# Two-layer hybrid decoder on one core: S5 products on different rows and columns of TensorE, and the Mamba-2 step-size chain in PSUM

## The chip, the cores and the metric

The kernel runs on one core of a Trainium2 chip. The engines of a core run side by side, each with its own in-order list of instructions, and wait for each other on semaphores: TensorE (PE) multiplies, VectorE (DVE) and GpSimd (POOL) do elementwise work, ScalarE (ACT) does activations and copies, SyncE (SP) issues DMAs. The metric is the device time of the whole program in microseconds (us); lower is better.

## The reference, cut to what matters

```python
D_MODEL, SEQ, DEPTH = 1024, 512, 2
for l in range(DEPTH):
    h = rmsnorm(x, ln1_g[l]); proj = h @ w_in[l]
    o_a = diff_attention(q, k, v, ...)                 # 4 heads, q and k normed and rotated
    o_b = sc_b * causal_dwconv(sc_c * sc_h, sc_conv_w[l])
    o_c = s5_mixer(proj[..., OFF_S5:OFF_M2Z], ...)
    o_d = mamba2_mixer(z, xbc, dt_raw, ...)
    x = x + concat(o_a, o_b, o_c, o_d) @ w_out[l]
    h2 = rmsnorm(x, ln2_g[l])
    x = x + (silu(causal_dwconv(h2 @ ffn_w_gate[l])) * (h2 @ ffn_w_up[l])) @ ffn_w_down[l]

def s5_mixer(u, ...):                    # 16 groups of 16 channels, 64 complex states each
    bu = einsum('bsgh,gph->bsgp', u, b_bar)            # input product, real and imaginary part
    xs = associative_scan(a2*a1, a2*x1 + x2)           # along the 512 positions
    y = einsum('bsgp,ghp->bsgh', xs, c).real + d_skip * u   # output product
    g = gelu(y); return g * sigmoid(g @ w_glu + b_glu)

def mamba2_mixer(...):
    xbc = silu(causal_dwconv(xbc, conv_w) + conv_b)
    dt = softplus(dt_raw + dt_bias)                    # the step sizes: 512 positions x 4 heads
    y = ssd_chunked(xs * dt, a * dt, bm, cm); ...
```

## The kernel before, in words

Activations lie transposed: 128 channels on the partitions, 512 positions along the row. Every large product is cut into *units*: one unit is 128 output channels. Its weights are fetched by SP (`raw`), split by ACT into a high part (`wh`, line 697, `prep`) and by POOL into the rest (`wl`, line 287, `low`), and multiplied by PE in three groups of products (lines 386, 388, 396), of which the last needs `wl`. `raw`, `wh` and `wl` have two buffers each, so ACT can split the weights of a unit only when PE has read the high part of the unit two before it. A layer has 28 units of the input projection, then attention with the first output units among it, eight units for the rest of the output projection, and 60 units of the gated MLP.

The input projection is a hand-written schedule. Each engine has a loop over the step `s` from 2 (ACT from 1) to 27, where step `s` is unit `s`, and small pieces of the four mixers are put at fixed steps of each loop. What the change touches:

- **Mamba-2 convolution, steps 2 to 7.** DVE scales the unit out of its bank (line 942) and runs four taps in the bank (lines 959 to 962); ACT then applies Silu from the bank (line 790) in the same step, after `prep()`. Between them, in steps 2 to 4, DVE computes the softplus of the step sizes on tiles of 16 columns: `m2_dt`, `m2_log`, `m2_series` (lines 1019 and 1021, seven dependent operations) and `m2_steps`. All of these tiles lie in SBUF, in `s16` (`s` in the trace).
- **S5, eight steps `j`.** `s5_in(j)` on PE makes two products, real into bank 2 and imaginary into bank 3, both from the same 32 rows of `u` (line 437). DVE turns them by a cosine/sine table and scans them (`s5_scan`, lines 1130 to 1144), ACT copies both out (line 772), DVE makes the real part `sE` (`s5_back`, lines 1151 to 1160) and POOL the imaginary part `s5im` (lines 320 to 324). `s5_out(j)` on PE adds real (line 446) and imaginary (line 448) into the same 32 rows of bank 6. `s5_in(j + 1)` needs bank 2 back, that is `sE` of step `j`. POOL may write `s5im` again when PE has read it, and makes the tables (lines 301 to 311) when DVE has done with the old ones.
- **q and k, steps 17 to 24.** `qk_mean` on PE (lines 531 and 533), the reciprocal root on ACT as Ln then Exp (lines 715 and 717), `qk_finish` on DVE (lines 1260 to 1265), whose last operation frees bank 5 for the next line 533.
- **Attention, 16 steps `n`.** Scores on PE (lines 553 to 557; the two products of a pair use rows 0 to 63 and 64 to 127, and go to two banks), maxima and combination on DVE (lines 1272 to 1281), Exp on ACT (line 832). Once per head there is an Ln (line 842) and an Exp (line 846).

ACT holds one set of function tables at a time. A table load is an instruction in its list, put there when the next function isn't in the set that is loaded.

## Time and profile before

| | us |
|---|---|
| median of 3 runs | 1472.79 |
| lowest, highest | 1471.87, 1472.96 |
| the profiled execution, its own time | 1473.24 |
| its span, first to last instruction | 1471.4 |
| mean granted TensorE clock, share of full | 0.977 |

The 1.8 us between the span and the time lie around the program and are the same for both kernels. In a timeline row the first number is the start, the second the time from that start to the last end of the merged instructions; neighbouring groups of matmuls overlap a little, so what a group costs on PE is the start of the next group less its own start. A value in brackets is the idle time ahead, and who ended it. A product of fp32 operands shows as two matmuls.

### The profile page before, as it was taken

To read this page: it belongs to the slowest core of one execution; us is meant where nothing else is said; L and a number is where in the kernel's file an instruction comes from. 1 tells how busy PE (TensorE), PEld (TensorE's weight loads), DVE (VectorE), ACT (ScalarE), POOL (GpSimd) and SP (SyncE) were. 2 spreads that over 40 slices of the span, in tenths; PEclk is the share of its full clock that TensorE was granted. 3 is DMA by queue.
4 is the path that set the end of the run, shared out by engine and by line. 5 is a ranking of instruction groups with operands and counts; after the bars stand their busy time and mean duration, and the time that the engine had idled before them with its cause. 6 is when DMAs were issued, how large, how long until landed. Compare 5 with 4: busy or idle time off the path is not lost.

```text
span 1471.4 us, 15836 instructions
## 1 busy us (share of the span) xinstructions
PE 1395.4 (95%) x6116; PEld 1074.4 (73%) x6116; DVE 943.8 (64%) x1221; ACT 569.9 (39%) x805; POOL 685.7 (47%) x368
## 2 busy tenths in 40 slices
PE   3989999798999999999999999998899999999999
PEld 1777656476788888888877775665677888888887
DVE  7778887564677713777228788865657774067740
ACT  3342556456532312222333335645664332123221
POOL 1645768312444443444456456862134444444452
PEclk9999989999999999999999998998999999999999
DMA  5221111111332332323232211111123333223332
GB/s 185 71 73 58 44 53 55 36 33 33 107 101 92 111 98 87 95 91 116 85 100 72 61 55 58 52 42 33 40 54 112 99 100 118 83 86 101 104 101 97
DMA packets 33627, 117.41 MB, mean 80 GB/s; under 512 B 3728, under 2 KB 3856, under 8 KB 33552
## 3 DMA queue, kind: packets, MB, share of 16 engines
q1 hardware_dynamic: 33264, 115.35, 24.9%
q8 instruction: 49, 0.80, 0.2%
q10 hardware_dynamic: 288, 1.05, 0.2%
q14 instruction: 26, 0.21, 0.0%
HBM read 114.28 MB, written 2.10 MB: 79 GB/s over the span
## 4 chain that ended last, share of the span: by engine, by line
PE 84%; DVE 10%; ACT 3%; issue 2%; DMA 1%; POOL 1%; SPq 0%; DVEq 0%; POOLq 0%
PE bank L386 25%; PE bank L388 24%; PE bank L396 24%; PE bank L437 2%; DVE s L1021 1%; PE bank L533 1%; PE bank L448 1%; DVE ml L967 1%; PE bank L446 1%; PE bank L415 1%; PE bank L531 1%; DMA raw<-in_w_first 1%; DVE G L1281 1%; PE bank L572 1%; DVE xl L933 1%
## 5 line engine op out<-in xcount | busy, mean ns | idle before, releaser
L287 POOL TENSOR_TENSOR wl<-raw,wh 128x1024 fp32r<-128x1024 f32 (+3 forms) x208 | 501.7, 2413 | 679.5 <-ACT wh L697 458.5
L386 PE MATMUL bank<-xl,wh 128*128 128x512 f32 x1152 | 303.4, 404 | 35.8 <-ACT wh L697 24.9
L386 PEld LDWEIGHTS bank<-xl,wh 128*128 128x128 f32 x1152 | 217.8, 192 | 109.7 <-issue 39.7
L697 ACT ACTIVATE wh<-raw 128x1024 fp32r<-128x1024 f32 (+3 forms) x208 | 218.3, 1050 | 196.9 <-PE bank L388 191.2
L388 PE MATMUL bank<-xh,wh 128*128 128x512 f32 x1152 | 287.9, 392 | 0.0
L396 PE MATMUL bank<-xh,wl 128*128 128x512 f32 x1152 | 286.1, 390 | 0.0
L388 PEld LDWEIGHTS bank<-xh,wh 128*128 128x128 f32 x1152 | 218.5, 190 | 46.1
L396 PEld LDWEIGHTS bank<-xh,wl 128*128 128x128 f32 x1152 | 216.4, 188 | 45.2 <-issue 0.3
L971 DVE TENSOR_TENSOR x<-x,bank 128x512 f32<-128x512 f32 x64 | 44.0, 687 | 219.7 <-PE bank L396 219.7
L386 PE MATMUL bank<-ml,wh 128*128 128x512 f32 x512 | 136.3, 408 | 0.0
L388 PE MATMUL bank<-mh,wh 128*128 128x512 f32 x512 | 128.4, 391 | 0.0
L396 PE MATMUL bank<-mh,wl 128*128 128x512 f32 x512 | 127.5, 389 | 0.0
L386 PEld LDWEIGHTS bank<-ml,wh 128*128 128x128 f32 x512 | 97.8, 194 | 24.5 <-issue 3.0
L388 PEld LDWEIGHTS bank<-mh,wh 128*128 128x128 f32 x512 | 96.9, 189 | 20.9
L396 PEld LDWEIGHTS bank<-mh,wl 128*128 128x128 f32 x512 | 96.1, 188 | 20.0
L1303 DVE TENSOR_TENSOR G<-G 128x512 f32<-128x512 f32 x44 | 105.2, 2391 | 4.6
L893 ACT ACTIVATE G<-G 128x512 f32<-128x512 f32 x44 | 27.8, 632 | 204.4 <-DVE G L954 204.4
L949 DVE TENSOR_SCALAR G<-pad,par_all 128x512 f32<-128x512 f32 x48 | 94.3, 1964 | 1.5
L942 DVE TENSOR_TENSOR G<-bank,rbc 128x512 f32<-128x512 f32 x76 | 52.2, 687 | 63.7 <-PE bank L396 61.4
L942 DVE TENSOR_TENSOR pad<-bank,rbc 128x512 f32<-128x512 f32 x60 | 41.4, 691 | 53.9 <-PE bank L396 43.3
L896 ACT ACTIVATE mh<-G 128x512 fp32r<-128x512 f32 x44 | 27.7, 630 | 111.1 <-DVE G L1303 111.1
L1305 DVE TENSOR_TENSOR ml<-G,mh 128x512 fp32r<-128x512 f32 x44 | 47.3, 1074 | 31.2 <-ACT mh L896 31.2
(264 smaller groups left out, 1529.9 us busy)
## 6 DMA issues: line engine op xcount, KB each, us to landing
raw<-in_w_gu SPq DMA_DIRECT2D x88, 512.0 KB, 3.5
raw<-in_w_in SPq DMA_DIRECT2D x52, 512.0 KB, 3.5
raw<-in_w_dn SPq DMA_DIRECT2D x32, 704.0 KB, 4.1
raw<-in_w_oe SPq DMA_DIRECT2D x16, 384.0 KB, 3.0
raw<-in_w_ol SPq DMA_DIRECT2D x16, 256.0 KB, 2.6
x<-in_x SPq DMA_DIRECT2D x8, 256.0 KB, 6.1
raw<-in_w_first SPq DMA_DIRECT2D x4, 512.0 KB, 6.7
out_x<-x SPq DMA_DIRECT2D x8, 256.0 KB, 4.7
```

What stands on the lines that cost most here:

```text
L287: tt(wl[:, p, 0:cols], raw[:, p, 0:cols], wh[:, p, 0:cols].bitcast(F32), ALU.subtract).then_inc(wl_full, 1)
L386: mm(bank[b][:, :], wh[:, p, k * P:(k + 1) * P], lo[:, k, :], start=(k == 0), stop=False)
L388: w = mm(bank[b][:, :], wh[:, p, k * P:(k + 1) * P], hi[:, k, :], start=False, stop=False)
L396: w = mm(bank[b][:, :], wl[:, p, k * P:(k + 1) * P], hi[:, k, :], start=False, stop=(k == K - 1))
L437: mm(bank[2 + c][:, :], bmat[r:r + SH, c, j // 4, :], u[r:r + SH, j // 4, :], start=True, stop=True).then_inc(dve_bank[2 + c], 1)
L697: fn(wh[:, p, 0:cols], raw[:, p, 0:cols], ACT.Copy).then_inc(wh_full, 1)
L893: fn(G[:, 1, :], G[:, 0, :], ACT.Silu).then_inc(g_silu, 1)
L942: tt(out, bank[b][:, :], rbc[:, :], MUL).then_inc(unit_out, 1)
L949: after(ts(out, pad[:, p, 4:4 + T], weights[n - 1], None, MUL))
L971: tt(x[:, o, :], x[:, o, :], bank[p][:, :], ADD).then_inc(resid, 1)
L1303: tt(G[:, 3, :], G[:, 1, :], G[:, 2, :], MUL).then_inc(h_ready, 1)
L1305: tt(ml[:, i, :], G[:, 3, :], mh[:, i, :].bitcast(F32), SUB).then_inc(hid_ready, 1)
```

## The change

- `s5_in`: the imaginary product now reads a second copy of `u` whose partition halves are exchanged (`uswap`, two DMAs per layer on SP after step 5's weights), with `bmat` rolled to match. The two products of a step so use rows `r` and `r + 64` of the array.
- `s5_out(j)`: the real product of step `j` is followed by the imaginary product of step `j - 1`; the two write different groups of 32 rows of the bank, so use different columns of the array. `s5im` gets a second buffer. The last imaginary product stands alone behind `s5_out(7)`. Bank 7 takes the sums of `j` from 4 up. The first Gelu and the sum ahead of it go from step 21 to 23.
- The step-size chain keeps one operand of nearly every operation in PSUM (`small(i)`, columns of bank 5).
- ACT's Silu of a convolved unit stands one step later, behind the `prep()` of the next weights.
- `ln_exp_tables()` loads one set of tables with Ln and Exp at five places; the loads between each Ln and Exp are no longer in the list.

```diff
@@ sync
+                if g % (len(UNITS) // L) == 5:
+                    sp.wait_ge(unit_out, unit_out_of(l, 1))
+                    for to, of in ((0, P // 2), (P // 2, 0)):
+                        sp.dma_start(uswap[to:to + P // 2, :, :], u[of:of + P // 2, :, :]).then_inc(u_swapped, 16)
@@ gpsimd, s5_imaginary
-                if j:
-                    pool.wait_ge(s5_summed, l * SJ + j)
-                tt(s5im[:, :], sB[:, :], sn, ALU.mult)
+                if j > 1:
+                    pool.wait_ge(s5_summed, l * SJ + j - 1)
+                im = imag[j % 2][:, :]
+                tt(im, sB[:, :], sn, ALU.mult)
@@ tensor
+                    pe.wait_ge(u_swapped, 32 * (l + 1))
                 r = SH * (j % 4)
-                for c in range(2):
-                    claim(2 + c, (s5x_ready, dve_free[3])[c])
-                    mm(bank[2 + c][:, :], bmat[r:r + SH, c, j // 4, :],
-                       u[r:r + SH, j // 4, :], start=True, stop=True).then_inc(dve_bank[2 + c], 1)
+                claim(2, s5x_ready)
+                claim(3, dve_free[3])
+                for c, (rows, first) in enumerate(((u, r), (uswap, (r + P // 2) % P))):
+                    at = slice(first, first + SH)
+                    mm(bank[2 + c][:, :], bmat[at, c, j // 4, :], rows[at, j // 4, :],
+                       start=True, stop=True).then_inc(dve_bank[2 + c], 1)
...
             def s5_out(j):
...
+                if j:
+                    pe.wait_ge(s5im_ready, nth(s5im_ready))
+                s5_real(j)
+                if j:
+                    s5_imag(j - 1)
@@ scalar
+            def ln_exp_tables():
+
+                nc.scalar.preload_act_table_set("natural_log_exp_and_others")
...
-                    if 2 <= s <= 7:
+                    if 3 <= s <= 8:
                         act.wait_ge(conv_out, nth(conv_out))
-                        fn(xbc[:, s - 2, :], bank[unit_bank(s)][:, :], ACT.Silu).then_inc(xbc_silu, 1)
-                    if s == 6:
+                        fn(xbc[:, s - 3, :], bank[unit_bank(s - 1)][:, :], ACT.Silu).then_inc(xbc_silu, 1)
+                    if s == 7:
@@ vector
+            def small(i):
+
+                return bank[5][:, 32 + 16 * i:48 + 16 * i]
...
             def m2_series():
-                sq, q = [s16[:, i, :] for i in (9, 10)]
+                sq, q = s16[:, 9, :], small(2)
                 dve.wait_ge(dve_own, owned())
                 after(ts(q, sq, 1.0 / 17, None, MUL))
                 for c in (15, 13, 11, 9, 7, 5, 3):
...
-                stt(u[:, i, :], u[:, i, :], par_of(l, "s5d", i), bank[6][:, :], MUL, ADD).then_inc(y_ready, 1)
+                stt(u[:, i, :], u[:, i, :], par_of(l, "s5d", i), bank[6 + i][:, :], MUL, ADD).then_inc(y_ready, 1)
```

PE's list in the steps with q and k, before and then with the change (lines 437, 446, 448 are 449, 458, 463 in the new numbering; 531 and 533 are 554 and 556):

```order
L437 MATMUL bank<-u,bmat 128x512 x2
L386 MATMUL bank<-xl,wh 128x512 x8
L388 MATMUL bank<-xh,wh 128x512 x8
L396 MATMUL bank<-xh,wl 128x512 x8
L531 MATMUL bank<-G,cst 128x512
L533 MATMUL bank<-G,permg 128x512
L446 MATMUL bank<-s5e,cf 32x512
L448 MATMUL bank<-s5im,cf 32x512
L386 MATMUL bank<-xl,wh 128x512 x8
```

```order
L449 MATMUL bank<-u,bmat 128x512
L449 MATMUL bank<-uswap,bmat 128x512
L395 MATMUL bank<-xl,wh 128x512 x8
L397 MATMUL bank<-xh,wh 128x512 x8
L405 MATMUL bank<-xh,wl 128x512 x8
L554 MATMUL bank<-G,cst 128x512
L556 MATMUL bank<-G,permg 128x512
L458 MATMUL bank<-s5e,cf 32x512
L463 MATMUL bank<-s5i,cf 32x512
L395 MATMUL bank<-xl,wh 128x512 x8
```

The places and the number of products are the same; the second of each pair reads another tile, and the imaginary one (`s5i` is the second buffer of `s5im`) is that of the step before.

ACT's list in steps 1 to 4 of the input projection, before and after (697 is `prep`, 787 the exponential of the step sizes, 790 Silu; now 722, 818, 821):

```order
L697 ACTIVATE wh<-raw 128x1024 x2
L787 ACTIVATE s_102<-s_102 128x16
L790 ACT_TABLE_LOAD
L790 ACTIVATE xbc<-bank 128x512
L697 ACTIVATE wh<-raw 128x1024
L790 ACTIVATE xbc<-bank 128x512
L697 ACTIVATE wh<-raw 128x1024
L790 ACTIVATE xbc<-bank 128x512
```

```order
L722 ACTIVATE wh<-raw 128x1024 x2
L818 ACTIVATE s_104<-s_104 128x16
L722 ACTIVATE wh<-raw 128x1024
L821 ACT_TABLE_LOAD
L821 ACTIVATE xbc<-bank 128x512
L722 ACTIVATE wh<-raw 128x1024
L821 ACTIVATE xbc<-bank 128x512
```

One more split of weights now stands ahead of the first Silu, and so ahead of each later one.

## Rows read from the trace of the kernel before

**Rows 1.** The page, busy time and share of the span of each engine.

```profile
PE 1395.4 (95%) x6116; PEld 1074.4 (73%) x6116; DVE 943.8 (64%) x1221; ACT 569.9 (39%) x805; POOL 685.7 (47%) x368
```

**Rows 2.** Timeline of PE: start, us, instructions, idle before; layers 0 and 1.

```profile
80.61 3.78 PE L386 MATMUL bank<-xl,wh 128*128 128x512 f32 x8 [4.20 <-ACT wh L697]
...
799.05 3.66 PE L386 MATMUL bank<-xl,wh 128*128 128x512 f32 x8 [2.66 <-ACT wh L697]
```

**Rows 3.** Stretches: length, busy of PE, PEld, DVE, ACT, POOL; granted clock, DMA.

```profile
80.60:86.80 6.20, 6.20 (x16) 4.88 (x17) 5.95 (x9) 1.54 (x2) 4.22 (x2) 0.58 0.29 87
...
188.00:262.00 74.00, 74.00 (x252) 45.99 (x251) 57.47 (x80) 41.25 (x49) 59.92 (x43) 0.95 0.15 48
```

**Rows 4.** Timeline of ACT: the Silu ahead of the weight split that PE waited for.

```profile
79.01 0.60 ACT L790 ACTIVATE xbc<-bank 128x512 f32<-128x512 f32 x1 [11.37 <-DVE bank L962]
```

**Rows 5.** Lines 1021 and 961 on DVE: minimum, median, maximum in ns.

```profile
L1021 DVE SCALAR_TENSOR_TENSOR s<-s x14: 174/973/2424, 68.0 to 793.2; 128x16 f32<-128x16 f32 x14
...
L961 DVE SCALAR_TENSOR_TENSOR bank<-pad,par_all,bank x24: 754/756/757, 56.9 to 809.2; 128x512 f32<-128x512 f32 x24
```

**Rows 6.** Timeline of PE: the S5 products in steps 22 to 24, layer 0.

```profile
237.40 1.04 PE L446 MATMUL bank<-s5e,cf 128*32 128x512 f32 x2
238.28 1.02 PE L448 MATMUL bank<-s5im,cf 128*32 128x512 f32 x2
239.24 2.11 PE L386 MATMUL bank<-xl,wh 128*128 128x512 f32 x8
...
246.62 1.98 PE L437 MATMUL bank<-u,bmat 32*128 32x512 f32 x4
248.53 2.11 PE L386 MATMUL bank<-xl,wh 128*128 128x512 f32 x8
```

**Rows 7.** Timeline of PE: attention scores, 384 and 128 columns, and what follows.

```profile
287.37 0.92 PE L553 MATMUL bank<-qk 64*128 64x384 f32 x4
288.12 0.39 PE L555 MATMUL bank<-qk 64*128 64x128 f32 x4
...
313.83 0.49 PE L553 MATMUL bank<-qk 64*128 64x128 f32 x4
314.16 0.39 PE L555 MATMUL bank<-qk 64*128 64x128 f32 x4
```

**Rows 8.** Timeline of PE, layer 0, steps 18 and 19.

```profile
185.42 2.08 PE L533 MATMUL bank<-G,permg 128*128 128x512 f32 x2 [2.14 <-DVE qk L1265]
187.43 3.78 PE L437 MATMUL bank<-u,bmat 32*128 32x512 f32 x4
191.14 3.78 PE L386 MATMUL bank<-xl,wh 128*128 128x512 f32 x8
```

**Rows 9.** Timeline of DVE: ahead of 185 us, and the S5 real part of step 23.

```profile
177.15 3.38 DVE L967 TENSOR_TENSOR ml<-xbc,mh 128x512 fp32r<-128x512 f32 x2 [1.55 <-ACT mh L726]
180.46 2.85 DVE L1260 SCALAR_TENSOR_TENSOR qk<-G,par_all,rotary 128x512 f32<-128x512 f32 x1
...
245.19 0.69 DVE L1160 TENSOR_TENSOR s5e<-s5a,bank 128x512 f32<-128x512 f32 x1
```

**Rows 10.** Line 715 on ACT: the table loads, 22 of 84 in all.

```profile
L715 ACT ACT_TABLE_LOAD  x22: 1283/1283/1283, 45.3 to 1114.7; - x22
```

**Rows 11.** Timeline of PE: end of the projection, layer 0.

```profile
278.50 1.04 PE L448 MATMUL bank<-s5im,cf 128*32 128x512 f32 x2 [1.76 <-POOL s5im L324]
280.39 0.80 PE L553 MATMUL bank<-qk 64*128 64x128 f32 x4 [0.84 <-DVE u L1164]
```

**Rows 12.** Timeline of POOL, the same stretch.

```profile
274.61 1.27 POOL L320 TENSOR_TENSOR s5im<-s5b,ex 128x512 f32<-128x512 f32 x1 [11.64 <-PE bank L448]
```

**Rows 13.** Timeline of ACT: the last copy that POOL needs there.

```profile
270.77 0.60 ACT L772 ACTIVATE s5b<-bank 128x512 f32<-128x512 f32 x1 [0.51 <-DVE bank L1144]
```

**Rows 14.** Timeline of PE in attention, layer 0, at two head boundaries.

```profile
324.96 0.44 PE L563 MATMUL bank<-cst,G 128*128 128x128 f32 x2 [1.59 <-DVE G L1281]
...
343.06 0.44 PE L563 MATMUL bank<-cst,G 128*128 128x128 f32 x2 [1.61 <-DVE G L1281]
...
346.16 0.90 PE L563 MATMUL bank<-cst,G 128*128 128x128 f32 x3 [1.09 <-DVE G L1281]
```

More of the change, by code:

```diff
@@ L135, in build @@
         s5im = sb("s5im", [P, T], at=offsets["xds"])
+        imag = (s5im, s5im2)
         hst = sb("hst", [P, NQ - 1, M2H, M2P])
@@ L323, in s5_imaginary @@
                 pool.wait_ge(s5w_read, l * SJ + j + 1)
-                tt(s5im[:, :], s5im[:, :], s5t[:, :], ALU.add).then_inc(s5im_ready, 1)
+                tt(im, im, s5t[:, :], ALU.add).then_inc(s5im_ready, 1)
                 temp_free.append((s5im_ready, l * SJ + j + 1))
@@ L994, in dt_scaled @@
                 freed(dve_free[5])
+            def small(i):
+                return bank[5][:, 32 + 16 * i:48 + 16 * i]
             def m2_dt(l):
-                a, e = [s16[:, i, :] for i in (0, 1)]
+                a, e, raw_dt = s16[:, 0, :], s16[:, 1, :], small(0)
                 by_head = [P, NQ, M2H]
                 dve.wait_ge(dve_bank[5], nth(dve_bank[5]))
-                tt(a.rearrange("p (a b) -> p a b", a=NQ), bank[5][:, 0:16].rearrange("p (a b) -> p a b", a=NQ),
-                   par_of(l, "dtb", 0, M2H).unsqueeze(1).broadcast_to(by_head), ADD).then_inc(dve_free[5], 1)
-                dve.wait_ge(dve_free[5], freed(dve_free[5]))
-                stt(e, a, -1.0, a, MUL, ALU.max).then_inc(dt_abs, 1)
-                own(ts(a, a, 0.0, None, ALU.max))
+                for out in (a, raw_dt):
+                    w = tt(out.rearrange("p (a b) -> p a b", a=NQ), bank[5][:, 0:16].rearrange("p (a b) -> p a b", a=NQ),
+                           par_of(l, "dtb", 0, M2H).unsqueeze(1).broadcast_to(by_head), ADD)
+                after(w)
+                stt(e, raw_dt, -1.0, a, MUL, ALU.max).then_inc(dt_abs, 1)
+                dve.wait_ge(dt_abs, l + 1)
+                own(ts(a, raw_dt, 0.0, None, ALU.max))
             def m2_log():
-                e, s, sq, rec = [s16[:, i, :] for i in (1, 2, 9, 11)]
+                e, s, sq, rec = s16[:, 1, :], s16[:, 2, :], s16[:, 9, :], small(1)
                 dve.wait_ge(dt_exp, nth(dt_exp))
@@ L1012, in m2_log @@
                 after(nc.vector.reciprocal(rec, rec))
[L1013 to L1014 removed]
+                tt(s, e, rec, MUL)
+                after(tt(rec, e, rec, MUL))
+                own(tt(sq, rec, s, MUL))
             def m2_series():
[L1017 removed]
+                sq, q = s16[:, 9, :], small(2)
                 dve.wait_ge(dve_own, owned())
@@ L1023, in m2_steps @@
             def m2_steps():
-                a, s, q = [s16[:, i, :] for i in (0, 2, 10)]
+                a, s, q = s16[:, 0, :], s16[:, 2, :], small(2)
                 by_head = [P, NQ, M2H]
@@ L1028, in m2_steps @@
                 after(stt(q, q, 1.0, s, ADD, MUL))
-                after(stt(a, q, 2.0, a, MUL, ADD))
+                stt(a, q, 2.0, a, MUL, ADD).then_inc(dve_free[5], 1)
+                dve.wait_ge(dve_free[5], freed(dve_free[5]))
                 stt(adt.rearrange("p (a b) -> p a b", a=NQ), a.rearrange("p (a b) -> p a b", a=NQ), -1.0,
```

35 lines of the change are left out of this document (23 added, 12 removed).

## The prediction

> **What bounds the kernel now.** I read the page first: PE is busy for 95% of the span and no other engine for more than 64% [rows 1]. So time is won only where PE works less, waits less, or runs at a higher clock. Next I listed PE's idle gaps over the whole span in its timeline. Outside the first 31 us they lie at the same places in both layers: one ahead of 80.61 us (4.20 us; 2.66 us in layer 1) [rows 2], one of 1.7 near 147 (DVE's work on unit 13; nothing in the change touches it), two ahead of 185.42 [rows 8], the end of the projection [rows 11], and attention [rows 14]. After the long ones the granted clock is at its lower level for a while, 1.2 instead of 2.4 GHz: 0.58 of full speed on average from 80.6 to 86.8 [rows 3]. The MLP units have none of these gaps and are left out. Between 188 and 262 us PE has no gap at all, while DVE is busy for 57.5 and POOL for 59.9 of 74 us [rows 3]: there PE's own work counts, as long as the other two keep up.
>
> **The gap at 80.61: chain in PSUM, Silu one step later.** PE waits for ACT's split of its weights; ahead of that ACT had stood 11.37 us for the convolution, to run the Silu at 79.01 [rows 4]. DVE was late because of the series of line 1021. Its operations on 16 columns take 174 ns at best and 973 ns in the median, 2424 at worst, while the 512-column taps of line 961, which have one operand and the result in PSUM, take 754 to 757 ns in all 24 cases, with POOL busy beside them [rows 5]. A tiny operation slower than a 32 times larger one waits for something, and the row that is immune has only one SBUF operand. So I take 0.2 us for each of the seven, about 5 us less on DVE per layer. The Silu move gives another unit of room (5.5 us: 7.38 from 239.24 to 246.62 less two fp32 products of 0.9 [rows 6]) even without this. I count the whole gap, 4.20, and what the low clock costs: the 6.2 us from 80.6 ran at a mean clock of 0.58 [rows 3], and are 3.6 at full, so 2.6. Layer 1: 2.66, and one group of 8 products at 3.66 [rows 2] against 1.98 elsewhere, so 1.7. Together **11.1 us**. Next late would be DVE's own 4.6 us per unit, still under PE's 5.5. The later Silu holds a bank for some us longer, but four banks rotate here.
>
> The rule behind this is in the Trainium skill, page "SBUF — State Buffer", section "Who interferes with whom": a DVE instruction with two SBUF inputs contends with a GpSimd instruction that reads SBUF, one with at most one doesn't. By that rule the chain also stops holding POOL up. The trace agrees as far as the two groups of durations go.
>
> **Input products.** Four matmuls of line 437 occupy PE from 246.62 to 248.53, 1.91 us [rows 6]. The nearest row of two products on different rows of the array is that of the scores: four matmuls of 384 columns take 0.75 us (287.37 to 288.12), of 128 columns 0.33 (313.83 to 314.16) [rows 7]. A fp32 product of 512 columns costs 0.88 alone (237.40 to 238.28 [rows 6]), so 0.22 per 128 columns: in turn, 384 columns would take 1.3. They do overlap. From 0.33 and 0.75 the line goes on to 0.96 at 512 columns, so a pair saves 1.91 - 0.96 = 0.95 us. That row has 64 rows of the array and not 32; the bounds are 0 and 0.95, and I take 0.95, since the structure is the same (two row groups, two banks). Which of the eight pairs of a layer count: the one at 163.8 not (DVE is the bound right behind it, below); that at 187.43 runs at the low clock, 3.78 us [rows 8], and saves half, some 1.85; the other six 0.95 each. That makes 7.55 per layer, **15.1 us**.
>
> **Output products.** Real and imaginary of one step share the same 32 columns of the array now, 0.88 and 0.96 us (237.40, 238.28, 239.24 [rows 6]). With the change they use different columns. No row of before has two products side by side on different columns: 0 to 0.86 saved per pair. I take 0.86, because the row pairs overlap fully. Pairs that count: those of j = 2 to 5, so 3.44, and the first call at 128 us, which now issues one product instead of two, 0.86. The pair of j = 1 is lost in front of 185.42. That is 4.3 per layer, **8.6 us**. The Trainium skill, page "TensorEngine Tiling (Array Packing)", section "Key Properties", has a rule that speaks against both: to change the tiling mode drains the engine. The rows show something of the kind now: the eight products of line 386 take 2.11 us behind small ones [rows 6], and 1.98 elsewhere. By the rule this stays, since the switches are as many as before; by the rows too.
>
> **What must keep up.** `s5_in` needs `sE` of the step before: line 1160 ends at 245.88 (245.19 + 0.69 [rows 9]), PE comes at 246.62: 0.74 us of room, while a period of two units is to shrink by 1.8 us. But DVE is late there by ACT, which runs two table loads of 1.283 us around each Ln [rows 10]; 54 of 84 loads go, two of them here, 2.57 us. That turns the room into about 1.5 us over the first period, and it doesn't shrink afterwards, as DVE's scan starts from PE's product and moves with it. POOL's work in a period of 18.5 us is 15.0 (59.9 of 74 [rows 3]) against 16.7 of PE then, and it no longer waits for PE's reading of `s5im`.
>
> **Steps 16 to 18.** PE's wait of 2.14 us [rows 8] and one of 1.5 ahead of it hang on one chain: m2_norm, Ln and Exp on ACT, then DVE to line 1265. DVE spends 3.38 on two operations of line 967 and 2.85 on line 1260 [rows 9], all with two SBUF operands beside a busy POOL; these stay. Of the chain one load goes, 1.28. PE arrives 3 us earlier than now but waits the longer: **2.6 us** for two layers, low clock kept.
>
> **End of the projection.** Line 448 waits 1.76 us for POOL, which could start only at 274.61 when PE had read the buffer [rows 11, 12]; ACT had copied the data by 271.37 [rows 13]. With two buffers POOL ends near 275.2. Then bank 2 is next: scores can't start before `sE` of the last step, 274.5. From there: scores, v turn, pair (0.98), last imaginary (0.9), sum on DVE, scores at about 278.5 instead of 280.39 [rows 11]: 1.9 per layer, **3.8 us**.
>
> **Attention.** ACT loads tables ahead of and behind each Ln (2.57 us), and PE waits for what follows: 1.59 us at the first boundary, which goes whole, and 1.61 and twice 1.09 at the last [rows 14]. Those 3.8 us become about 2.3, since maxima and exponentials of the next scores take their time anyway. That is 1.59 + 1.5 = 3.1 per layer, **6.2 us**. I leave the low clock behind it as it is.
>
> **Priced at nothing**: the two uswap DMAs (issued in step 5, needed in step 10; what SP waits for, unit 1's output, is written before step 2, so no weights are held back), the Gelu two steps later, bank 7 for half of the sums (free from step 16), one more operation of 0.2 us on DVE.
>
> **Sum.** 11.1 + 15.1 + 8.6 + 2.6 + 3.8 + 6.2 = 47.4. From the profiled 1473.24 that gives 1425.8; the median is 0.45 below the profiled execution, so **1425.5 us**.
>
> **Rivals.**
> - *Low-clock stretches in attention and at the projection's end go too* as the gaps ahead of them shrink (3.4 us of loss behind 346 in each layer, as much around 282 and 998): 8 to 10 us more, 1416; with those behind 185 also, 10 more, 1406. Against: gaps of 2.6 us in 4 were enough at 277 to 280.
> - *Columns don't overlap*: 8.6 and some 1.7 at the end come back, 1435.8. For: no row shows it. Against: rows of the array do overlap.
> - *DVE or POOL becomes the bound in steps 18 to 26*: three input pairs and four output pairs per layer are lost, 2 x (2.85 + 3.44) = 12.6, so 1438. For: the 0.74 us of room, and that lines 1260 and 967 lengthen beside POOL. Against: the freed table loads.
> - *Rows don't overlap for 32-row products*: 15.1 back, 1440.6.
> - *Slower*: POOL, freed from waiting, runs beside every line 1260 (2.85 instead of 0.74 [rows 9]); DVE's period then passes 18.5 us, PE gets a gap per period, and each drops the clock as at 185 (10 us, loss 5). With four such in each layer, 40 us, and the 12.6 lost: 1478. It decides from 4 us more DVE time in each period than now.
>
> **How the numbers follow.** Forecast 0.50, low clock gone 0.18, columns 0.13, DVE or POOL 0.12, rows 0.04, slower 0.02, and 0.01 for gains that cancel out. The range, 1408 to 1440, holds all but the last three and the far end of the first rival. A measurement of this kernel can tell 0.2%, 2.9 us, from no change: faster 0.97, same 0.01, slower 0.02.
>
> **What would show it.** No gap ahead of unit 7 near 76 us in either layer, and the counterpart of line 1021 at 0.2 us; the input pair at 0.96 us and the output pair at 0.98 instead of 1.91 and 1.84; a PE without gaps and with periods of 16.7 us between 190 and 250; a longer single wait ahead of line 533 at the start of that; 30 table loads in all. A gap ahead of `s5_in` in steps 20 to 26 would prove the engines' rival, an output pair of 1.8 us that of the columns. The forecast falls if gains pass PE but come back as waits for DVE.

## The result, and the profile after

| | before | after |
|---|---|---|
| median, us | 1472.74 | 1415.13 |
| lowest, highest of 4 runs each | 1471.87, 1472.96 | 1414.43, 1416.61 |
| span of the profiled execution | 1471.4 | 1414.8 |
| mean granted TensorE clock | 0.977 | 0.990 |

The ratio is 0.9611, with a 95% interval of 0.9595 to 0.9628: 57.6 us less. The forecast was 1425.5 in a range from 1408 to 1440, so 47.4 of those 57.6 us were seen ahead, and 10.2 us weren't.

The page of after, busy time of each engine and share of the span:

```profile
PE 1352.1 (96%) x6116; PEld 1057.2 (75%) x6116; DVE 920.0 (65%) x1225; ACT 500.5 (35%) x751; POOL 685.4 (48%) x368
```

Against [rows 1], PE has the same 6116 instructions and is busy for 43.3 us less: pairs that overlap, and less time at the low clock. ACT has 54 instructions fewer, the table loads.

**The step-size chain.** The seven operations of the series (line 1061 now), with minimum, median and maximum in ns, where they take 174/973/2424 in [rows 5]:

```profile
L1061 DVE SCALAR_TENSOR_TENSOR bank<-bank,s x14: 182/182/182, 67.2 to 758.6; 128x16 f32<-128x16 f32 x14
```

PE has no idle time left ahead of unit 7 in either layer, where [rows 2] have 4.20 and 2.66 us.

**The pairs.** Timeline of PE of after, steps 21 to 23 of layer 0 (start, time to the last end, instructions):

```profile
212.95 0.69 PE L449 MATMUL bank<-u,bmat 32*128 32x512 f32 x1
212.96 0.69 PE L449 MATMUL bank<-uswap,bmat 32*128 32x512 f32 x1
213.48 0.59 PE L449 MATMUL bank<-u,bmat 32*128 32x512 f32 x1
213.49 0.59 PE L449 MATMUL bank<-uswap,bmat 32*128 32x512 f32 x1
214.01 2.14 PE L395 MATMUL bank<-xl,wh 128*128 128x512 f32 x8
...
221.43 0.62 PE L458 MATMUL bank<-s5e,cf 128*32 128x512 f32 x1
221.44 0.62 PE L463 MATMUL bank<-s5i,cf 128*32 128x512 f32 x1
221.88 0.59 PE L458 MATMUL bank<-s5e,cf 128*32 128x512 f32 x1
222.41 2.11 PE L395 MATMUL bank<-xl,wh 128*128 128x512 f32 x8
...
229.81 0.69 PE L449 MATMUL bank<-u,bmat 32*128 32x512 f32 x1
```

The first matmuls of the two products start 10 ns apart, and so do the second ones. An input pair takes 1.06 us (212.95 to 214.01) instead of 1.91, an output pair 0.98 (221.43 to 222.41) instead of 1.84 [rows 6]. The period of two units is 16.86 us (212.95 to 229.81), where it was 18.52.

**What PE waits for now.** PE of after has ten waits of more than 0.7 us between the startup and 330 us. Three of them lie outside what the change aims at (0.96 us ahead of 116.38, 1.67 ahead of 140.15, 1.77 ahead of 252.66); the other seven, with the idle time ahead and what ended it in brackets:

```profile
174.15 1.13 PE L556 MATMUL bank<-G,permg 128*128 128x512 f32 x2 [2.34 <-DVE qk L1306]
176.07 1.15 PE L449 MATMUL bank<-u,bmat 32*128 32x512 f32 x1 [0.80 <-DVE s5e L1201]
255.27 0.49 PE L578 MATMUL bank<-qk 64*128 64x128 f32 x4 [1.00 <-DVE s5e L1201]
258.35 1.05 PE L463 MATMUL bank<-s5i,cf 128*32 128x512 f32 x2 [0.94 <-POOL s5i L333]
260.32 0.49 PE L576 MATMUL bank<-qk 64*128 64x128 f32 x4 [0.93 <-DVE u L1205]
270.15 0.49 PE L578 MATMUL bank<-qk 64*128 64x128 f32 x4 [1.68 <-ACT G L864]
319.85 0.55 PE L586 MATMUL bank<-cst,G 128*128 128x128 f32 x3 [1.23 <-DVE G L1322]
```

The wait at step 18 is the longest one: 2.34 us where [rows 8] have 2.14. Of the waits at head boundaries [rows 14] only one of 1.23 us is left.

**Where the 57.6 us went.** The starts of the same piece of work in both timelines cut each layer into segments. The startup differs by 0.8 us between the two profiled executions (it ends anywhere between 35.7 and 37.7 us in the kernels here), and is taken out.

| segment of a layer | layer 0 | layer 1 | both | forecast, both |
|---|---|---|---|---|
| up to the first turn of Mamba-2 (gap ahead of unit 7) | 6.9 | 4.6 | 11.5 | 11.1 |
| on to the S5 input product of step 16 | 1.9 | 2.0 | 3.9 | 5.5 |
| on to that of step 18 | 3.3 | 3.2 | 6.5 | 2.6 |
| on to that of step 26 | 7.2 | 7.0 | 14.2 | 16.3 |
| on to the scores | 1.6 | 1.5 | 3.1 | 5.7 |
| attention, up to the second norm | 9.0 | 9.2 | 18.2 | 6.2 |

The MLP has the same length in both (360.3 us from the second norm of layer 0 to the first of layer 1). Four rows are within 0.4 to 2.6 us of their term; step 16 to 18 gave 3.9 us more, and attention 12.0 more. The two rows that say why, PE's busy time and the granted clock in attention: length, PE, PEld, DVE, ACT, POOL busy, clock, DMA share, GB/s. Before:

```profile
280.40:396.30 115.90, 105.33 (x539) 80.48 (x540) 71.37 (x127) 70.23 (x141) 27.68 (x17) 0.93 0.18 55
997.00:1113.60 116.60, 106.51 (x538) 80.95 (x539) 71.92 (x128) 70.25 (x140) 28.29 (x18) 0.91 0.19 54
```

And after:

```profile
260.30:367.20 106.90, 100.33 (x539) 77.45 (x540) 69.36 (x127) 59.93 (x133) 27.69 (x17) 0.97 0.20 59
950.00:1057.00 107.00, 100.41 (x538) 77.52 (x539) 69.48 (x128) 60.08 (x132) 27.93 (x17) 0.97 0.19 59
```

For the same matmuls PE is idle for 6.6 us instead of 10.6 in layer 0, 4.0 less (the forecast had 3.1), and busy for 5.0 us less, at a clock of 0.97 instead of 0.93. In layer 1 it is 3.1 less idle (the stretch of before begins 0.4 us earlier in a wait, which is taken out) and 6.1 less busy. So 7.1 us are waits, and 11.1 are matmuls that no longer run at 1.2 GHz. Before had three stretches at 1.2 GHz in each layer there, in layer 0 from 280.3 (the projection's end), 294.0 and 345.4 (the last head boundary); after has only the middle one, from 271.9. The place of the first one in layer 0, before and after:

```profile
280.00:287.00 7.00, 6.61 (x29) 3.97 (x29) 4.29 (x12) 5.18 (x9) 1.98 (x2) 0.76 0.38 115
260.00:267.00 7.00, 6.04 (x31) 3.29 (x33) 4.39 (x12) 5.41 (x10) 1.83 (x2) 1.00 0.42 115
```

### The profile page after: what moved, and what is told of

The parts are those of the page before. It is cut to its first block, busy times and chain, and to the rows that moved or that the text cites. A ratio compares the mean times of both kernels' runs of the same rounds, so it can differ in the third digit from the quotient of the medians.

```text
span 1414.8 us, 15816 instructions
## 1 busy us (share of the span) xinstructions
PE 1352.1 (96%) x6116; PEld 1057.2 (75%) x6116; DVE 920.0 (65%) x1225; ACT 500.5 (35%) x751; POOL 685.4 (48%) x368
## 4 chain that ended last, share of the span: by engine, by line
PE 89%; DVE 7%; ACT 1%; issue 1%; DMA 1%; POOL 1%; SPq 0%; DVEq 0%; POOLq 0%
PE bank L395 26%; PE bank L397 26%; PE bank L405 26%; PE bank L449 1%; PE bank L595 1%; PE bank L458 1%; PE bank L424 1%; PE bank L554 1%; PE bank L556 1%; PE bank L576 1%; DMA raw<-in_w_first 1%; PE bank L586 1%; DVE xl L966 1%; DVE ml L1000 1%; PE bank L478 0%
## 5 line engine op out<-in xcount | busy, mean ns | idle before, releaser
L295 POOL TENSOR_TENSOR wl<-raw,wh 128x1024 fp32r<-128x1024 f32 (+3 forms) x208 | 500.5, 2407 | 650.4 <-ACT wh L722 408.4
L395 PE MATMUL bank<-ml,wh 128*128 128x512 f32 x512 | 133.4, 402 | 0.0
L1344 DVE TENSOR_TENSOR G<-G 128x512 f32<-128x512 f32 x44 | 109.3, 2484 | 4.6
```

The costliest lines, as they stand in the source:

```text
L295: tt(wl[:, p, 0:cols], raw[:, p, 0:cols], wh[:, p, 0:cols].bitcast(F32), ALU.subtract).then_inc(wl_full, 1)
L395: mm(bank[b][:, :], wh[:, p, k * P:(k + 1) * P], lo[:, k, :], start=(k == 0), stop=False)
L1344: tt(G[:, 3, :], G[:, 1, :], G[:, 2, :], MUL).then_inc(h_ready, 1)
```

## The experiments

Times are medians in us; the interval is that of the ratio to the kernel before. The last column is an estimate of what the low clock costs in the profiled execution: its span times (1 - mean granted clock), with the clock as the trace has it, before it is rounded. The kernel before is at 1.2 GHz for 68.3 us, so 34.1. One profiled execution need not be the median one: that of u_cols was the fastest of its four and had a clock of 0.998, the other three 0.995.

| kernel | median | ratio, interval | to after | span, clock | low clock costs |
|---|---|---|---|---|---|
| after | 1415.1 | 0.9611, 0.9595 to 0.9628 | | 1414.8, 0.990 | 13.7 |
| b_tables: before and five preloads | 1445.9 | 0.9817, 0.9803 to 0.9830 | +30.8 | 1442.8, 0.989 | 15.4 |
| u_tables: without preloads | 1442.0 | 0.9792, 0.9776 to 0.9809 | +26.9 | 1441.3, 0.983 | 23.9 |
| u_chain: chain in SBUF | 1424.4 | 0.9676, 0.9661 to 0.9690 | +9.3 | 1422.7, 0.989 | 15.4 |
| u_silu: Silu in its old step | 1415.8 | 0.9618, 0.9604 to 0.9631 | +0.7 | 1413.7, 0.990 | 13.7 |
| u_both: chain and Silu as before | 1422.8 | 0.9660, 0.9646 to 0.9673 | +7.7 | 1420.4, 0.989 | 15.4 |
| u_rows: input products on the same rows | 1424.9 | 0.9677, 0.9663 to 0.9691 | +9.8 | 1423.0, 0.992 | 11.9 |
| n_near: rows 32 apart | 1416.7 | 0.9619, 0.9605 to 0.9632 | +1.5 | 1415.0, 0.990 | 13.7 |
| u_cols: output products on the same columns | 1415.3 | 0.9612, 0.9597 to 0.9626 | +0.2 | 1412.0, 0.998 | 3.4 |
| m_emit: DVE's splits of step 17 later | 1406.3 | 0.9553, 0.9539 to 0.9566 | -8.8 | 1403.8, 0.995 | 6.8 |
| m_emit_cols: that, and same columns | 1411.5 | 0.9587, 0.9574 to 0.9600 | -3.7 | 1410.1, 0.995 | 6.8 |
| m_emit_rows: that, and same rows | 1415.5 | 0.9613, 0.9600 to 0.9626 | +0.4 | 1413.4, 0.995 | 6.8 |
| m_mix: m_emit, and another move on DVE | 1411.4 | 0.9585, 0.9572 to 0.9598 | -3.7 | 1410.3, 0.992 | 11.9 |

### Table loads

*u_tables*, the changed kernel with the loads between each Ln and Exp again, 84 in all:

```diff
             def ln_exp_tables():
-                nc.scalar.preload_act_table_set("natural_log_exp_and_others")
+                return
```

> The changed kernel without the five preloads of the set with Ln and Exp: the table loads come back to 84. Theory A (the loads are worth what the prediction gave them: 1.3 us at steps 16 to 18 and 3.1 in attention per layer): 9 us more, 1424. Theory B (with shorter chains the low-clock stretches in attention and before it vanish too, worth 1.7 to 3.4 us each): 18 to 24 us more, 1433 to 1439, and low clock behind the last head boundary as in the kernel before. Theory C (beside B, steps 20 to 26 become bound by ACT's rsqrt, so that input pairs wait for s5e): above 1440.

It took 26.9 us more. At 1442.0 that is theory C, and the wait for `sE` in steps 20 to 26 that it names is there, though only once per layer (0.88 us). From step 16 to step 18 it takes 23.7 us, as before, against 20.3 without the loads: this whole segment is the tables' (3.4 us per layer). PE has two waits there again. For the first, 3.27 us ahead of 174.21, two loads lie on the way to `G`. ACT's timeline:

```profile
169.71 1.28 ACT L740 ACT_TABLE_LOAD   x1
171.00 0.69 ACT L740 ACTIVATE G<-bank,cst 128x512 f32<-128x512 f32 x1
171.71 1.28 ACT L742 ACT_TABLE_LOAD   x1
173.54 0.61 ACT L794 ACTIVATE G<-G 128x512 f32<-128x512 f32 x1
```

But the second wait, ahead of 177.42, ends last, and it is for DVE's `qk` (line 1306). On its chain there is one load, at 156.53, ahead of `z`. DVE's timeline of u_tables:

```profile
158.50 2.75 DVE L1431 SCALAR_TENSOR_TENSOR xbc<-xbc,par_all,z 128x512 f32<-128x512 f32 x2 [2.44 <-ACT z L742]
...
169.21 3.34 DVE L1000 TENSOR_TENSOR ml<-xbc,mh 128x512 fp32r<-128x512 f32 x2 [1.55 <-ACT mh L756]
172.47 2.83 DVE L1301 SCALAR_TENSOR_TENSOR qk<-G,par_all,rotary 128x512 f32<-128x512 f32 x1
```

And of after:

```profile
157.23 2.75 DVE L1431 SCALAR_TENSOR_TENSOR xbc<-xbc,par_all,z 128x512 f32<-128x512 f32 x2 [1.19 <-ACT z L742]
...
167.95 2.40 DVE L1000 TENSOR_TENSOR ml<-xbc,mh 128x512 fp32r<-128x512 f32 x2 [1.55 <-ACT mh L756]
170.26 1.77 DVE L1301 SCALAR_TENSOR_TENSOR qk<-G,par_all,rotary 128x512 f32<-128x512 f32 x1
```

Both startups end at 37.4 us, so the times can be compared. DVE begins 1.3 us later with the load, and the same two lines then take 2.0 us longer. Layer 1 shows the same (3.35 and 2.84 against 2.41 and 1.77). The two lines lie beside other POOL operations then, since POOL isn't late by as much; that this is what stretches them was not tried.

In steps 18 to 26 the loads add 1.6 us, two small gaps at 231.94 and 234.80, and in attention 8.1. Unit 7 isn't touched. Together that is 13.1 us per layer. The low clock costs 23.9 - 13.7 = 10.2 of the 26.9 us.

*b_tables* is the other side: the kernel before, with the five preloads and nothing else.

```diff
+            def ln_exp_tables():
+                nc.scalar.preload_act_table_set("natural_log_exp_and_others")
             def rms():
+                ln_exp_tables()
```

(and four more calls, at the places where the changed kernel has them.)

> The kernel before with the five table preloads alone, 30 loads instead of 84. Theory from the run without them (27 us above the changed kernel, which includes about 6 us of waits that arise only with PE's faster S5 products): 1472.7 less 19 to 23, 1450 to 1454; waits at the head boundaries gone, low clock behind 346 us gone. Rival (the loads' worth hangs on the other parts; alone they bring the 9 us of the prediction): 1464.

It took 1445.9, 26.6 us less than before, more than either theory had. The low clock costs 15.4 instead of 34.1 us: 70% of the gain are clock. PE's timeline of b_tables has these waits at the places of [rows 8] and, in layer 1, of [rows 2]; of those of [rows 14] it has one of 1.23 us, as after:

```profile
179.43 1.12 PE L533 MATMUL bank<-G,permg 128*128 128x512 f32 x2 [1.01 <-DVE qk L1273]
181.36 1.98 PE L437 MATMUL bank<-u,bmat 32*128 32x512 f32 x4 [0.80 <-DVE s5e L1168]
...
784.11 3.62 PE L386 MATMUL bank<-xl,wh 128*128 128x512 f32 x8 [2.66 <-ACT wh L697]
```

The products at 179.43 and 181.36 run at 2.4 GHz, where those of [rows 8] take nearly twice as long. The 2.66 us ahead of unit 7 in layer 1 are there still. In layer 0, however, the 4.20 us of [rows 2] are gone although the chain lies in SBUF as before:

```profile
75.44 1.98 PE L396 MATMUL bank<-xh,wl 128*128 128x512 f32 x8
77.35 2.11 PE L386 MATMUL bank<-xl,wh 128*128 128x512 f32 x8
```

The series takes 5.11 us there, where before it takes 7.74; in layer 1 it takes 7.84 in both. PE waits 1.94 us in all for DVE a little later, so layer 0 is 4.1 us ahead at the first S5 input product. Why the series was shorter wasn't tried: ACT has the scale of the norm ready earlier, and DVE and POOL meet at other times.

### The step-size chain and the Silu

*u_chain* and *u_silu* undo one of the two each, *u_both* undoes both.

```diff
@@ u_chain, u_both
             def small(i):
-                return bank[5][:, 32 + 16 * i:48 + 16 * i]
+                return s16[:, (10, 11, 10)[i], :]
@@ u_silu, u_both
-                    if 3 <= s <= 8:
+                    if 2 <= s <= 7:
-                        fn(xbc[:, s - 3, :], bank[unit_bank(s - 1)][:, :], ACT.Silu)
+                        fn(xbc[:, s - 2, :], bank[unit_bank(s)][:, :], ACT.Silu)
```

> The changed kernel with the step-size chain back in SBUF only, Silu still one step later. Theory (both parts are needed: DVE comes some 6 us later, and what is next late is the turn of unit 7, whose second bank waits for DVE's copy of the sums behind the convolution of unit 6): 4 us more per layer and perhaps a low-clock stretch, 8 to 14 us more, 1423 to 1429. Rival (the Silu move alone covers the gap ahead of unit 7): within 2 us of the changed kernel.

> The changed kernel with ACT's Silu of steps 2 to 7 back in its old step, chain in PSUM. Theory (the PSUM chain alone takes DVE's lateness away, so that the Silu of unit 4 comes at 72.5 us, its weights at 73.5, and PE needs them at 77): within 1.5 us of the changed kernel. Rival (the Silu move carries part of the gain): 3 us or more above it, with a wait for ACT's split ahead of unit 7 or 8.

> The changed kernel with two parts undone together: the step-size chain back in SBUF and ACT's Silu back in its old step. Alone, the chain costs 9.3 us (1424.4) and the Silu nothing (1415.8). Theory A, the Silu's later step is cover that matters only when DVE is late: with the slow chain PE now waits for the weights of unit 7 as in the kernel before, 4 us in layer 0 and 2.7 in layer 1 instead of 2.6 and 2.6 us and 1.2 ahead, and the time is 1 to 6 us above 1424.4, so 1425 to 1430. Theory B, the two parts are independent: 1424 to 1425, since the gap is DVE's lateness alone. Neither: below 1420.

u_chain took 9.3 us more, as expected. The operations of the series in it:

```profile
L1061 DVE SCALAR_TENSOR_TENSOR s<-s x14: 175/974/2323, 67.4 to 770.4; 128x16 f32<-128x16 f32 x14
```

These are the figures of [rows 5] again. The one thing that differs from after is where the tiles lie, so the operands' place is the cause of the slow series. PE then waits, though not where it did before:

```profile
83.80 0.66 PE L493 MATMUL bank<-cst,xbc 128*128 128x128 f32 x4 [1.17 <-ACT xbc L821]
87.08 1.11 PE L493 MATMUL bank<-cst,xbc 128*128 128x128 f32 x4 [2.62 <-DVE s L1209]
```

With the Silu a step later, the weights of unit 7 are there in time, but the turns of Mamba-2 wait 3.8 us in layer 0 instead, 1.17 for the Silu's result and 2.62 for DVE's copy of the sums (line 1209), and in layer 1 for that copy alone, 2.62. With the Silu in its old step too (u_both), PE waits 1.31 us for unit 7's weights in layer 0 and 1.84 in layer 1:

```profile
77.60 2.11 PE L395 MATMUL bank<-xl,wh 128*128 128x512 f32 x8 [1.31 <-ACT wh L722]
...
771.07 3.14 PE L395 MATMUL bank<-xl,wh 128*128 128x512 f32 x8 [1.84 <-ACT wh L722]
```

The medians are 1422.8 and 1424.4, with intervals that overlap; 1422.8 is 1 to 2 us below what either theory had. So the Silu's move is worth nothing that these runs can tell, with the fast chain (0.7 us, intervals overlap) or with the slow one: it moves a wait from unit 7 to the turns. Theory A of u_both is refuted. With the slow chain the comparison is coarse: the series took 7.75 and 5.60 us in the two layers of u_chain and 6.11 and 7.02 in those of u_both.

### Input products on different rows

*u_rows* puts both products back on the same rows; *n_near* keeps two row groups, but neighbouring ones; *m_emit_rows* is u_rows where step 18 has no wait (m_emit, below).

```diff
@@ u_rows, m_emit_rows
-                for c, (rows, first) in enumerate(((u, r), (uswap, (r + P // 2) % P))):
+                for c, (rows, first) in enumerate(((u, r), (u, r))):
-    bmat[:, :, 1] = np.roll(bmat[:, :, 1], P // 2, axis=1)
@@ n_near
-                    for to, of in ((0, P // 2), (P // 2, 0)):
+                    for to, of, n in ((SH, 0, P - SH), (0, P - SH, SH)):
...
-                for c, (rows, first) in enumerate(((u, r), (uswap, (r + P // 2) % P))):
+                for c, (rows, first) in enumerate(((u, r), (uswap, (r + SH) % P))):
```

> The changed kernel with both input products of a step from the same rows of u again (imaginary weights not rolled); all else stays. Theory (the pair overlaps because its rows differ): each pair costs 1.9 us instead of 1.06, 0.85 us more at seven of eight places per layer, 1.7 at the one behind the low clock: some 14 us above the changed kernel, 1429. Rival (the pair is off the path, since DVE's scan or POOL is next in line): less than 5 us more, 1415 to 1420.

> The changed kernel with the second copy of u and the second half of bmat rotated by 32 partitions instead of 64, so that the two input products of a step use neighbouring groups of 32 rows of the array. Theory A, any two different groups of rows overlap: a pair still takes 1.06 us and the time is that of the changed kernel, 1414 to 1417. Theory B, only groups that are 64 rows apart overlap, as the score products do: a pair takes 1.9 us and the time goes to about 1424, as with the same rows.

> The version of 1406.3, without waits or low clock at step 18, with both input products of a step from the same rows again. It prices the input pairs where the low clock of step 18 can't mask them: seven pairs per layer at 1.91 - 1.06 = 0.85 us are 11.9 us, so about 1416 to 1418 if all lie on the path. Rival: as the columns (5.1 us instead of 9 to 11), half is given back by other waits or by less time at the low clock: 1411 to 1414.

u_rows took 9.8 us more, between its theory and its rival; the pair takes 1.91 us again:

```profile
214.47 1.98 PE L449 MATMUL bank<-u,bmat 32*128 32x512 f32 x4
216.38 2.11 PE L395 MATMUL bank<-xl,wh 128*128 128x512 f32 x8
```

Seven pairs per layer at 1.91 - 1.06 = 0.85 would be 11.9 us. The low clock costs 1.7 us less than in after, so without that the rows would be worth 11.5 (an estimate). In m_emit_rows, whose low clock costs the same as m_emit's, they are worth 9.2: less than theory A had, more than the rival. In n_near a pair takes 1.06 us:

```profile
213.26 0.69 PE L449 MATMUL bank<-u,bmat 32*128 32x512 f32 x1
213.26 0.69 PE L449 MATMUL bank<-uswap,bmat 32*128 32x512 f32 x1
...
214.32 2.14 PE L395 MATMUL bank<-xl,wh 128*128 128x512 f32 x8
```

Neighbouring groups of rows overlap as well as those 64 apart, and the time can't be told from after's.

### Output products on different columns

*u_cols* adds real and imaginary of the same step, one behind the other, into the same columns again (the second buffer and bank 7 stay); *m_emit_cols* does that on m_emit.

```diff
-                if j:
-                    pe.wait_ge(s5im_ready, nth(s5im_ready))
                 s5_real(j)
-                if j:
-                    s5_imag(j - 1)
+                pe.wait_ge(s5im_ready, nth(s5im_ready))
+                s5_imag(j)
```

> The changed kernel with real and imaginary output product of the same step side by side again, on the same columns, each waiting for its own operand; the second s5im buffer and bank 7 stay. Theory (columns overlap): 0.86 us more per pair for j = 1 to 7, the first one moved back beside (0.86), one lost ahead of the DVE-bound place: 6 to 7 us per layer, 1427 to 1429. Rival (most of the gain came from the second buffer and not from the columns): under 5 us in all, 1420 or less.

> The kernel with the moved low parts, and beside that the output products of a step on the same columns again, as in the run that came out at the changed kernel's time. Theory (there the pairs did save 0.86 us each, and the longer low-clock stretches behind the wait of step 18 ate it): with that wait gone the pairs show, 0.86 us for some six pairs per layer: 9 to 11 us above the kernel with the moved low parts alone, about 1412. Rival (columns bring nothing; PE isn't the bound there): within 2 us of it.

u_cols missed its expectation by 12 us: 1415.3, the time of after. That is in the rival's range, but not for the rival's reason: the pair takes 1.83 us in it, and its period in steps 18 to 24 is 17.7 us instead of 16.86. The two kernels around step 18, first u_cols (two rows of PE's timeline, then a stretch of 8 us in the columns of the stretches above):

```profile
173.35 1.12 PE L554 MATMUL bank<-G,permg 128*128 128x512 f32 x2 [1.55 <-DVE qk L1302]
175.28 0.69 PE L449 MATMUL bank<-u,bmat 32*128 32x512 f32 x1 [0.80 <-DVE s5e L1197]
```

```profile
176.00:184.00 8.00, 8.00 (x31) 5.32 (x30) 7.93 (x12) 0.49 (x1) 7.84 (x6) 1.00 0.04 16
```

Then after, the same stretch:

```profile
176.00:184.00 8.00, 7.93 (x20) 5.19 (x21) 7.93 (x13) 0.63 (x1) 7.84 (x7) 0.57 0.13 55
```

After does 20 matmuls in these 8 us, u_cols 31. The startup of u_cols ends 1.6 us earlier; with that taken out, PE comes 1.7 us later to the wait without pairs, waits 1.55 us instead of 2.34, and keeps its clock. With pairs it comes earlier, waits the longer, and then runs at 1.2 GHz for 6.8 of the 8 us, in both layers. That costs 3.4 us per layer, 6.8 in all; another 3.4 us of difference in the last column lie in attention, and by their clock of 0.995 the other three executions of u_cols don't have them.

Piece by piece in layer 0, the pairs win 0.9 us up to step 18, lose 2.4 from there to step 20 where they should win 0.84, win 2.5 in steps 20 to 26, and lose 1.1 from there to the scores. The sum is nothing (0.1 us in layer 1, by the same count). This is why the columns looked like nothing. The 1.1 us have a cause of their own: the order with pairs has one more imaginary product alone, and a wait for POOL ahead of it (0.94 us at 258.35 in after). POOL, which has two buffers now, still stands there until PE has read one:

```profile
254.46 1.27 POOL L329 TENSOR_TENSOR s5i<-s5b,ex 128x512 f32<-128x512 f32 x1 [9.00 <-PE bank L463]
```

The buffer's last reader is the imaginary product of two steps before, which the new order issues one step later. In u_cols, with the same two buffers, POOL starts when ACT's copy is there, and PE doesn't wait for it.

In m_emit, whose PE doesn't wait at step 18, the columns are worth 5.1 us, with equal clocks in both: half of what the theory of m_emit_cols had, and more than its rival. Up to the input product of step 26 it is 4.1 us in layer 0 (242.62 against 238.17, less 0.4 of startup), by the end of attention 2.7; most of the 1.4 us between them is the loss at the projection's end again.

### A version without the wait at step 18

In step 17 DVE runs two splits (line 1000) ahead of the q/k work and of `sE` (line 1201), for which PE waits. *m_emit* puts them behind:

```diff
-                    if s == 17:
-                        for i in range(2):
-                            emit_low(MIXD + i, xbc[:, 4 + i, :])
                     if 17 <= s <= 24:
                         qk_finish(l, s - 17)
...
                         (s5_back if s % 2 else s5_scan)(l, (s - 12) // 2)
+                    if s == 17:
+                        for i in range(2):
+                            emit_low(MIXD + i, xbc[:, 4 + i, :])
```

> The changed kernel with DVE's two low parts of the Mamba-2 output (line 1000, two SBUF inputs, 2.4 us for both, 1.55 us of waiting for ACT ahead) moved from ahead of the first qk_finish in step 17 to behind s5_back of the same step. Theory (the output products' gain was given back there: PE arrives earlier, waits 2.34 + 0.80 us in one stretch and then runs 6.8 us at the low clock): both waits and the low clock go, 3.1 + 3.4 us per layer, 13 us less, 1402. Rival (ACT's rsqrt or the contended line 1301 takes their place as last): 3 us less at most, 1412.

It took 1406.3, 8.8 us less than after and 66.4 less than before, the best of all here, between the 1402 of its theory and the 1412 of its rival. DVE's timeline of m_emit:

```profile
171.45 0.69 DVE L1201 TENSOR_TENSOR s5e<-s5a,bank 128x512 f32<-128x512 f32 x1
172.06 3.18 DVE L1000 TENSOR_TENSOR ml<-xbc,mh 128x512 fp32r<-128x512 f32 x2
```

`sE` is there at 172.1 instead of 176.0, both waits of step 18 are gone in both layers, and so is the low clock behind them (6.8 us less). New are waits of 0.47 and 0.22 us, at 187.99 and 190.19 in layer 0.

*m_mix* goes one step further: in step 13 Mamba-2's mixing (up to line 1272) is moved ahead of the short convolution's taps, for the wait of 1.67 us at 140.15.

```diff
-                        sc_conv(l, s % 2)
-                        m2_mix(s - 10)
+                        if s == 13:
+                            m2_mix(s - 10)
+                        sc_conv(l, s % 2)
+                        if s == 12:
+                            m2_mix(s - 10)
```

> The version of 1406.3 (DVE's two splits of step 17 behind the real part of S5) with a second move on DVE: in step 13 the last mixing operation of Mamba-2 stands ahead of the short convolution's taps instead of behind them. PE waits there for the unit's bank, 1.67 us at about 140 us of the span in each layer. Theory A, the wait is DVE's order alone: it goes or halves in both layers, 1402 to 1404.5. Theory B, what is late next (Gelu operands, POOL) takes its place: 1405.5 to 1407.5.

That wait did go in both layers, and the time rose by 5.1 us. PE's timeline of m_mix has this instead (and the same 3.65 us in layer 1):

```profile
157.51 0.69 PE L449 MATMUL bank<-u,bmat 32*128 32x512 f32 x1 [3.65 <-DVE s5e L1201]
```

In m_emit this input product starts at 155.44 with no wait. The reordered DVE waits 1.19 us for ACT ahead of line 1268, since it comes there earlier, and its line 1296 takes 2.17 us instead of 1.04; so it begins the S5 scan at 145.39 instead of 143.07, and `sE` is late by as much, while PE comes 1.7 us earlier. The input product is 1.9 us later in the end, and the low clock costs 5.1 us more than in m_emit. Both expectations fell: what is late next wasn't the Gelu or POOL, but DVE itself.

## Why the prediction was right, and where it was short

The time is inside the range, 10.4 us below the forecast of 1425.5, and the pairs, the chain in PSUM and the preloads each do what was forecast of them. Term by term:

- **Chain and Silu, 11.1 us: right in size (11.5), half right in cause.** Line 1061 takes 182 ns, as taken (0.2 us). Undoing the chain alone costs 9.3 us. The sentence that the Silu move "gives another unit of room even without this" is wrong: with the slow chain the time is the same with and without it. Nor is the gap of layer 0 the chain's alone: with the preloads and the slow chain (b_tables) it is gone too. The rule of the Trainium skill, page "SBUF — State Buffer", section "Who interferes with whom" (two SBUF inputs on DVE contend with a GpSimd instruction that reads SBUF) fits u_chain: 175 ns at best, 2323 at worst for the same operation, against 182 in all 14 cases with one operand and the result in PSUM. Which of the two counts, the operand or the result, no run separates.
- **Input pairs, 15.1: mechanism right, the saving of a pair off by a tenth, its worth to the kernel by a third.** A pair takes 1.06, not 0.96: its second matmuls start 0.53 us behind the first ones, where those of an output pair start 0.45 behind, and the line through 128 and 384 columns didn't show that. Undone alone they are worth 9.8, or 11.5 with the clock taken out, and 9.2 in m_emit. The 1.85 us for the pair at low clock nearly came: 1.95 us (176.07 to 178.02) instead of 3.71 [rows 8]. The pair of step 16 was priced at nothing since a wait follows, and that was right: without it (u_rows) the wait at step 18 is 1.39 instead of 2.34.
- **Output pairs, 8.6: mechanism right (0.98 us, as taken), worth 0 in this kernel and 5.1 in m_emit.** The forecast's step that failed is that gains which reach PE ahead of a wait cost nothing but the gain: here the longer wait was followed by 6.8 us at 1.2 GHz in each layer (8 us at a mean of 0.57), which u_cols hasn't. The order that makes the pairs also costs 1.1 us per layer at the projection's end, which the forecast had at nothing. The segment from step 18 to 26 still gave 14.2 of 16.3 us against before, because before had a low clock there as well.
- **Steps 16 to 18, 2.6: measured 6.5.** "Of the chain one load goes" was right: DVE begins 1.3 us earlier, 2.5 us in both layers. What failed is the sentence on lines 967 and 1260 (now 1000 and 1301), "these stay": they take 2.40 and 1.77 us in after, not 3.38 and 2.85, 2.1 us less per layer. That a longer single wait would remain (2.34) was right too.
- **End of the projection, 5.7 with the last input pair: measured 3.1.** "With two buffers POOL ends near 275.2" failed. POOL still waits for PE's reading there, since the order with pairs reads each buffer a step later, and PE waits 0.94 us for POOL. The forecast counted one wait from there to the scores; after has three of about 1 us each (255.27, 258.35, 260.32). In u_cols, with the second buffer but the old order, this segment is 1.1 us shorter still.
- **Attention, 6.2: measured 18.2.** This is the step that failed most, and it has the size of the whole miss. The waits shrank by 7.1 us (6.2 forecast), but "I leave the low clock behind it as it is" was wrong: the clock went from 0.93 and 0.91 to 0.97 in both layers and gave 11.1 us. That was the first rival, 1416, at a chance of 0.18; the time is 1415.1. The argument against it, that gaps of 2.6 us in 4 were enough at 277 to 280, didn't hold even for the place it was read from: after still has waits of 1.00, 0.94 and 0.93 us there, and no low clock behind them. Nor did it for the last head boundary. Why the stretch between the two stayed isn't shown. That the time lies within 1 us of this rival is luck in part: the other rows of the sum miss by up to 3.9 us, some too high and some too low, and cancel to 2.0. One of its readings was off as well: the stretch around 282 in layer 0 is 3.4 us long and so costs 1.7, not 3.4.
- **Did DVE or POOL become the bound?** Not between 180 and 250 us: PE is busy without a gap, DVE for 59.2 and POOL for 57.8 of 70 us:

```profile
180.00:250.00 70.00, 70.00 (x274) 46.88 (x273) 59.20 (x85) 26.45 (x37) 57.80 (x41) 0.98 0.18 57
```

- **The largest part was priced lowest.** The table loads are worth 26.6 us alone (4.1 of them by the shorter series in layer 0) and 26.9 undone, nearly half of the 57.6. By the forecast's own terms they were some 9 (steps 16 to 18, attention) and the room of DVE. Rule and row were both at hand: on the Trainium skill's page "ScalarE: Activation LUTs", section "Table sets: the hidden batching unit", Ln and Exp share one set. The trace agrees: with that set loaded ahead, the loads between them are gone, 54 at 1.283 us [rows 10], 69.3 us of ACT (busy 569.9 to 500.5). ACT is idle most of the time, so this busy time is no sum for PE; but loads at step 17 and at the head boundaries lie in chains that PE waits for, and 10.2 of the 26.9 us that they cost (18.7 of the 26.6) are clock.
- The parts undone one by one give 26.9 + 9.3 + 0.7 + 9.8 + 0.2 = 46.9 of 57.6 us. The remaining 10.7 belong to none of these parts alone. Some of it is the second buffer, which no run undoes: from step 26 to the scores u_cols takes 15.1 us against 17.8 before, of which the input pair is 0.85, so some 1.8 us per layer are left for the buffer and what was moved with it. Some is low clock and waits that several parts remove together, as the gap of layer 0. How the rest splits wasn't tried.

What stays open is what makes the granted clock fall. Waits of 2.34 and 0.80 us at step 18 were followed by 1.2 GHz in after, 1.55 and 0.80 weren't in u_cols, but 1.39 and 0.80 were in u_rows (its pair of four matmuls at 175.91 takes 2.54 us instead of 1.98). So the length of the wait alone doesn't decide it, and I can't say from these runs what does.

## What to carry to other kernels

List the table loads first and ask of each which wait it lies ahead of: preloading the one set with both functions was worth more than both changes to the matmuls together, and took one line at each of five places. When PE is at 95%, price a wait with the clock behind it, read the granted clock of each stretch before and after, and value a change to the matmuls in a version where no wait can swallow it (u_cols against m_emit_cols: 0.2 us and 5.1). A gain that PE reaches ahead of a wait can be worth nothing until DVE's order is changed too, and each such move has to be followed to DVE's next deadline (m_emit won 8.8 us, m_mix lost 5.1 of them).

## What the hardware showed that I had not expected

- Two fp32 products on different rows or different columns start within 10 ns of each other though they stand one behind the other in PE's list, and their four matmuls take 1.06 us (rows) and 0.98 us (columns) together, hardly more than the 0.88 us of one product alone. It makes no difference whether the row groups are 64 or 32 apart (1.06 us in both).
- Less work on PE needn't give a shorter time: u_cols has output products without overlap, and a median of 1415.3 against 1415.1 us, since a stretch of 6.8 us at 1.2 GHz in each layer of after is missing in it.
- The same two DVE operations with SBUF operands (lines 1000 and 1301) take 4.2 us in after and 6.2 in u_tables, where they begin 1.3 us later beside a busy POOL, and so in both layers. Moving DVE's start can change how long its operations take.
- An operation on 128x16 elements costs 175 to 2323 ns with its operands in SBUF while POOL works, and 182 ns in all 14 cases with one of them in PSUM.
